# Down projections of a feed-forward stage: which engine forms the weight block differences and adds the residuals

## The reference, cut to what matters

```python
x = x + rms_norm(mixed, norm_mix_post)
h = rms_norm(x, norm_ffn_pre)
f = (jax.nn.silu(h @ w_gate) * (h @ w_up)) @ w_down
x = x + rms_norm(f, norm_ffn_post)
# rms_norm(x, g) = x * rsqrt(mean(x * x, axis=-1) + EPS) * g
```

## Time and profile before

| | |
|---|---|
| median of 3 runs | 2623.14 us (2622.61 to 2630.82) |
| the profiled execution's own time | 2624.92 us |
| its span | 2623.1 us |
| TensorE busy | 2398.5 us, 91% |
| VectorE busy | 1660.0 us, 63% |
| ScalarE busy | 1204.3 us, 46% |
| GpSimd busy | 847.5 us, 32% |
| mean granted TensorE clock | 0.968 |

### The profile page before, as it was taken

One profiled execution on the slowest core, in us unless ns is written; L12 is line 12 of the kernel. 1 busy time (PEld: TensorE's weight loads), 2 busy tenths in 40 slices (PEclk: granted clock), 3 DMA queues, 4 the chain that ended last, 5 costly groups with the idle time before them and its releaser, 6 DMA issues. The chain is left out here.

```text
span 2623.1 us, 36658 instructions
## 1 busy us (share of the span) xinstructions
PE 2398.5 (91%) x11796; PEld 1986.3 (76%) x11796; DVE 1660.0 (63%) x2987; ACT 1204.3 (46%) x2731; POOL 847.5 (32%) x912
## 2 busy tenths in 40 slices
PE   7999988996888888799589999999999999999896
PEld 5888876885776767577468888888878888888785
DVE  5676775554888888333265556558776455456877
ACT  5555563332676666333243333335444333334353
POOL 1323322222565665344401111135210111114623
PEclk9999998997999999899799999999999999999998
DMA  5111122444132221465452323256664332327663
GB/s 174 45 51 55 51 77 83 131 131 154 58 101 77 76 77 34 165 216 198 148 228 89 116 97 108 81 178 224 232 241 149 103 114 89 117 81 261 230 230 118
DMA packets 222105, 340.08 MB, mean 130 GB/s; under 512 B 20320, under 2 KB 119648, under 8 KB 220128
## 3 DMA queue, kind: packets, MB, share of 16 engines
q1 hardware_dynamic: 221920, 337.86, 38.6%
HBM read 234.50 MB, written 103.28 MB: 129 GB/s over the span
## 5 line engine op out<-in xcount | busy, mean ns | idle before, releaser
L2402 PE MATMUL ff_psum<-ff_hop,ff_a_hi 128*128 128x512 f32 x1760 | 543.3, 390 | 4.8 <-issue 4.8
L2402 PEld LDWEIGHTS ff_psum<-ff_hop,ff_a_hi 128*128 128x128 f32 x1760 | 330.8, 188 | 75.0 <-issue 6.4
L2402 PE MATMUL ff_psum<-ff_hop,ff_a_lo 128*128 128x512 f32 x880 | 342.8, 390 | 0.0
L2426 PE MATMUL ff_psum<-ff_a_hi 128*128 128x512 f32 x616 | 243.1, 395 | 14.4 <-DVE ff_a_lo L2213 14.3
L2029 POOL TENSOR_TENSOR ff_go<-ff_go 128x512 f32<-128x512 f32 x22 | 28.4, 1291 | 669.4 <-DVE ff_go L2279 669.4
L2426 PE MATMUL ff_psum<-ff_a_lo,ff_a_hi 128*128 128x512 f32 x616 | 241.4, 392 | 0.0
L2426 PE MATMUL ff_psum<-ff_a_hi,ff_a_lo 128*128 128x512 f32 x616 | 241.4, 392 | 0.0
L2213 DVE TENSOR_TENSOR ff_a_lo<-ff_ring,ff_a_hi 128x512 fp32r<-128x512 f32 x220 | 207.7, 969 | 51.2 <-ACT ff_a_hi L2100 51.2
L2100 ACT ACTIVATE ff_a_hi<-ff_w_raw 128x512 fp32r<-128x512 f32 x220 | 137.7, 628 | 211.3 <-PE ff_psum L2402 189.1
L2402 PE MATMUL ff_psum<-hop,ff_a_hi 128*128 128x512 f32 x704 | 217.8, 391 | 17.0 <-DVE ff_a_lo L2213 17.0
L1222 ACT ACTIVATE da_probs<-da_psum,da_bias 128x512 f32<-128x512 f32 (+3 forms) x320 | 196.1, 622 | 72.9 <-DVE da_bias L1274 60.8
(11 more groups left out here) (235 smaller groups left out, 5492.8 us busy)
## 6 DMA issues: line engine op xcount, KB each, us to landing
g_s<-ff_go SPq DMA_DIRECT2D x154, 256.0 KB, 2.0
ff_ring<-g_s SPq DMA_DIRECT2D x154, 256.0 KB, 3.0
ff_ring<-in_w_down_dram SPq DMA_DIRECT2D x132, 256.0 KB, 3.7
ff_w_raw<-in_w_gate_dram SPq DMA_DIRECT2D x44, 512.0 KB, 3.6
ff_w_raw<-in_w_up_dram SPq DMA_DIRECT2D x44, 512.0 KB, 4.1
pp_x<-in_x_dram SPq DMA_DIRECT2D x32, 512.0 KB, 4.6
hop_s<-op_ht SPq DMA_DIRECT2D x8, 1792.0 KB, 7.6
ff_hop<-hop_s SPq DMA_DIRECT2D x10, 1024.0 KB, 9.9
```

The costliest lines, as they stand in the source:

```text
L2402: last = pe.matmul(ps[:, bank, :], w[:, unit % R, at], hop[i][:, h, c, :], start=(i in (0, 1, 6) and c == 0 and x_ == 0), stop=(c == 3 and ...
L2426: last = pe.matmul(ps[:, bank, :], g[:, unit % R, at], w[:, (unit + 1) % R, :], start=(i in (0, 1, 6) and c == 0 and x_ == 0), stop=(c == ...
```

## The change

`b_of` moves unchanged from GpSimd to VectorE, and is called in VectorE's down step `t` for step `t + 4`, after the two low parts of that step. `add_x` moves to VectorE as well. VectorE's extras no longer stand in runs of neighbouring steps: in pass 0 `hop_half` goes to steps 24, 26, 28, 30 and 59 to 62; in pass 1 `norm` of `y_back` to steps 12, 16, 20, 24 and its `add_x` to 14, 18, 22, 26; `norm` of `y2` to 63, 65, 69, 71 and its `add_x` to 64, 68, 70, 72; the four bank additions after step 43 go one to a step. ScalarE's squares of `y_back` go from steps 14 to 17 to steps 6 to 9, and so SyncE's loads of `y_back` and `x_back` stand after step 10 in place of 12; the stores of `y_back` stand after step 40 in place of 38, the loads for steps 59 to 62 after step 64 in place of 68. At the end of a pass two of the four stores of `y2` come behind the loads of step 76. In the last group the gain row is multiplied in beforehand (`scale`: the right half in steps 73 to 76, the left half after the last matmul), so that one scalar_tensor_tensor per tile, `y1 * rstd + x`, is left behind the reciprocal root.

```diff
@@ SyncE, down(p)
-                        if p == 1 and t == 12:
+                        if p == 1 and t == 10:
                             ...
-                        if p == 1 and t == 38:
+                        if p == 1 and t == 40:
                             store_rows(b.y_back, 0, 0, 1)
-                        if p == 0 and t == 68:
+                        if p == 0 and t == 64:
                             ...
-                    store_rows(y2, p, 1, 2 * p)
+                    store_rows(y2, p, 1, 2 * p, (0, 1))
                     load_step(p, DOWN - 1)
+                    store_rows(y2, p, 1, 2 * p, (2, 3))
@@ GpSimd (b_of and add_x removed)
-                    for t in range(NJ, 5 * NJ):
-                        b_of(p, t)
-                        if p == 1 and t == 27:
-                            rstd_of(1)
-                        if p == 1 and 28 <= t < 32:
-                            add_x(b.y_back, b.x_back, 1, t - 28)
+                    if p == 1:
+                        rstd_of(1)
                     rstd_of(2 * p)
-                    for k in range(4):
-                        add_x(y2, b.x_in, 2 * p, k)
@@ VectorE
+                def add_x(y, x, group, k):
+                    dve.wait_ge(x_loaded, 64 * group + 64)
+                    dve.wait_ge(y_normed, 4 * group + k + 1)
+                    dve.tensor_tensor(y[:, k, :], y[:, k, :], x[:, k, :], ALU.add).then_inc(x_added, 1)
+                def scale(n, k):
+                    at = slice(n * HT, (n + 1) * HT)
+                    dve.wait_ge(squared, 12 + 4 * (1 - n) + k + 1)
+                    dve.tensor_tensor(y1[:, k, at], y1[:, k, at], post_row[:, at], ALU.mult).then_inc(y_scaled, 1)
@@ VectorE, down_step(p, t), behind lo_until
+                    if NJ <= t + 4 < 5 * NJ:
+                        b_of(p, t + 4)
+                    if p == 1 and t in (12, 16, 20, 24):
+                        norm(b.y_back, 1, (t - 12) // 4)
+                    if p == 1 and t in (14, 18, 22, 26):
+                        add_x(b.y_back, b.x_back, 1, (t - 14) // 4)
+                    if t in (63, 65, 69, 71):
+                        norm(y2, 2 * p, (63, 65, 69, 71).index(t))
+                    if t in (64, 68, 70, 72):
+                        add_x(y2, b.x_in, 2 * p, (64, 68, 70, 72).index(t))
+                    if p == 1 and t >= 73:
+                        scale(1, t - 73)
@@ VectorE, behind the last bank additions
                 for k in range(4):
-                    norm(y1, 3, k)
-                    if k % 2 == 1:
-                        dve.wait_ge(last_x_loaded, 64)
-                        dve.wait_ge(y_normed, 12 + k + 1)
-                        dve.tensor_tensor(y1[:, k, :], y1[:, k, :], b.x_back[:, k, :], ALU.add).then_inc(dve_x_added, 1)
+                    scale(0, k)
+                    dve.wait_ge(rstd_ready, 3 + k + 1)
+                    dve.wait_ge(y_scaled, 4 + k + 1)
+                    dve.scalar_tensor_tensor(y1[:, k, :], y1[:, k, :], rstd[:, k:k + 1], b.x_back[:, k, :], ALU.mult, ALU.add)\
+                        .then_inc(x_added, 1)
```

More of the change, by code:

```diff
@@ L1817, in ffn @@
         squared, pool_step, rstd_ready = m.sem("squared"), m.sem("pool_step"), m.sem("rstd_ready")
-        y_normed, x_loaded, x_added, dve_x_added = (m.sem(n) for n in ("y_normed", "x_loaded", "x_added", "dve_x_added"))
+        y_normed, x_loaded, x_added, y_scaled = (m.sem(n) for n in ("y_normed", "x_loaded", "x_added", "y_scaled"))
         last_x_loaded = m.sem("last_x_loaded")
@@ L1955, in load_x, with store_rows @@
                         sp.dma_start(tile[:, k, :], x_mid[row(p, h, k):row(p, h, k) + P, :]).then_inc(semaphore, 16)
-                def store_rows(tile, p, h, group):
-                    for k in range(4):
+                def store_rows(tile, p, h, group, rows=range(4)):
+                    for k in rows:
                         sp.wait_ge(x_added, 4 * group + k + 1)
@@ L2013, in _ @@
                 for k in range(4):
-                    sp.wait_ge(*((x_added, 12 + k // 2 + 1) if k % 2 == 0 else (dve_x_added, k // 2 + 1)))
+                    sp.wait_ge(x_added, 12 + k + 1)
                     sp.dma_start(out[row(1, 0, k):row(1, 0, k) + P, :], y1[:, k, :]).then_inc(last_stored, 16)
@@ L2037, in a_of @@
                     pool.tensor_tensor(go[:, S4, :], go[:, C21, :], go[:, S2, :], ALU.subtract).then_inc(go_made, 1)
[L2039 to L2052, removed]
                 def rstd_of(group):
@@ L2058, in rstd_of @@
                     pool_rstd(pool, rstd[:, :], ss[:, 0, :], D, half[:, :], pool_step, group + 1).then_inc(rstd_ready, 1)
[L2060 to L2063, removed]
                 for p in range(PAIRS):
@@ L2084, in _ @@
                         .then_inc(rstd_ready, 1)
-                for k in (0, 2):
-                    add_x(y1, b.x_back, 3, k)
             @block.scalar
@@ L2164, in down_step @@
                             act.activation(to, ps[:, 4 + k, :], ACT.Copy).then_inc(y_copied, 1)
-                    if p == 0 and 24 <= t < 28:
-                        hop_half(1, 2 + (t - 24) // 2, t % 2)
-                    if p == 1 and 14 <= t < 18:
+                    if p == 0 and t in (24, 26, 28, 30):
+                        hop_half(1, 2 + (t - 24) // 4, (t - 24) // 2 % 2)
+                    if p == 1 and 6 <= t < 10:
                         act.wait_ge(y_loaded, 64)
-                        square(b.y_back, 1, t - 14)
+                        square(b.y_back, 1, t - 6)
                     if 57 <= t < 61:
@@ L2172, in down_step @@
                         square(y2, 2 * p, t - 57)
-                    if p == 0 and 67 <= t < 71:
-                        hop_half(1, (t - 67) // 2, (t - 67) % 2)
+                    if p == 0 and 59 <= t < 63:
+                        hop_half(1, (t - 59) // 2, (t - 59) % 2)
                     if p == 1 and 69 <= t < 73:
@@ L2221, in hop_half, with b_of @@
                         .then_inc(hop_split[i], 1)
+                def b_of(p, t):
+                    i, c = divmod(t, NJ)
+                    raw = ring[:, 2 * ring_at[t] + 1, :]
+                    dve.wait_ge(*step_at(p, t))
+                    if i in (1, 2):
+                        dve.wait_ge(*step_split(p, t - NJ))
+                        dve.tensor_tensor(keep[:, c, :], raw, keep[:, c, :], ALU.subtract).then_inc(b_made, 1)
+                    elif i == 3:
+                        dve.wait_ge(b_made, 4 * NJ * p + t - 2 * NJ + 1)
+                        dve.tensor_tensor(raw, keep[:, c, :], raw, ALU.subtract).then_inc(b_made, 1)
+                    else:
+                        dve.wait_ge(*step_split(p, t - 2 * NJ))
+                        dve.wait_ge(b_made, 4 * NJ * p + t - 2 * NJ + 1)
+                        dve.tensor_tensor(keep[:, c, :], raw, keep[:, c, :], ALU.subtract).then_inc(b_made, 1)
                 def s_of(p, j, x, v):
@@ L2292, in norm @@
                         dve.wait_ge(post_loaded, 16)
-                    dve.wait_ge(rstd_ready, group + 1 if group < 3 else 3 + k + 1)
+                    dve.wait_ge(rstd_ready, group + 1)
                     dve.scalar_tensor_tensor(y[:, k, :], y[:, k, :], rstd[:, k:k + 1], post_row[:, :], ALU.mult, ALU.mult)\
                         .then_inc(y_normed, 1)
+                def add_x(y, x, group, k):
[6 more added lines that the diff above has]
+                    dve.tensor_tensor(y1[:, k, at], y1[:, k, at], post_row[:, at], ALU.mult).then_inc(y_scaled, 1)
                 def add_c11(p, k):
@@ L2303, in down_step @@
                         up_slot(p, NJ - 1, 14 + t)
[L2304 to L2307, removed]
+                    if 4 * NJ <= t < 4 * NJ + 4:
+                        k = t - 4 * NJ
+                        dve.wait_ge(y_copied, 12 * p + 8 + k + 1)
+                        add_bank(y2[:, k, HT:D], k).then_inc(y_added, 1)
                     if t in (5 * NJ, 5 * NJ + 1):
```

1 line of the change is left out of this document (added).

## The result

The changed kernel takes 2593.62 us (median of 4 runs, 2591.81 to 2595.19), the kernel before 2625.89 us (4 runs, 2622.61 to 2630.82): ratio 0.988, 95% interval 0.9863 to 0.9898, so 27 to 36 us faster. The forecast was 2597 (2592 to 2605). The profiled execution took 2592.32 us, its span is 2590.5.

What follows compares the result with a forecast made beforehand. TensorE was taken as the bound, waiting in the down parts for VectorE's low parts; 21.0 us there plus 4.9 in the tail off the profiled 2624.92 gave 2599.0, less 1.8 for the median: 2597 us (2592 to 2605).

Steps and rivals of the forecast that it cites:

- The size of the loss: In the two down parts: time TensorE loses against its undisturbed pace, 6.0 and 15.0 us, all 21.0 us gained back.
- VectorE carries the load: In the down steps: VectorE takes the differences at 0.60 us each within 4.1 us of slack, cost 0.
- The queue move: Pass 1, earlier y_back and x_back loads: VectorE stands 3.7 us for step 11's load, 1.0 to spare, TensorE 0.
- The tail: After the last matmuls: first bank addition to last operation takes 11.5 us instead of 16.4, gain 4.9 us (3.3 to 6.5).
- the distance per tile: In the tail: time from one tile's last operation to the next, taken as 2.5 us (bounds 1.8 to 3.05).
- extras apart: Down parts: VectorE's side jobs no longer in neighbouring steps, counted within the 21.0 us gain without a price of its own.
- Rival B: Down parts: work moved from GpSimd still burdens VectorE, waits stay, only the tail gains, 2618 us; chance 0.05.
- A: Step 11 of pass 1 or hop halves of steps 59 to 62 land late: 1.8 to 6 us, 2601; chance 0.20.
- D: Pass 1: loads and VectorE wait for each other in a loop, 5 to 12 us, 2603 to 2609; chance 0.09.
- C: Down steps: VectorE becomes the bound at 3.15 us a step against 2.73, 37 us more, 2655; chance 0.04.

Runs made afterwards that it cites:

- e4: Changed kernel with 2.1 MB more loaded behind x_back and ahead of step 11 of pass 1; median 2602.91 us, ratio 0.9913 to the kernel before.
- e6: Changed kernel with one constant subtraction more on VectorE at each of its 88 differences; ratio 0.9901 to the kernel before.
- e1: Kernel before with the block differences moved to VectorE, norms still in neighbouring steps, additions still on GpSimd, tail as before; ratio 0.9975 to the kernel before.
- e2: Changed kernel with the block differences left on GpSimd and the tail as before; ratio 0.9926 to the kernel before.
- e5: Changed kernel with 88 more constant-block subtractions on GpSimd that nobody waits for; ratio 1.0022 to the kernel before.
- e10: Changed kernel with norms and x additions of y_back and y2 put back in neighbouring steps, both on VectorE; ratio 0.9918 to the kernel before.
- e7: Changed kernel with two constant subtractions more on VectorE at each of its 88 differences; ratio 1.0128 to the kernel before.

## Why the prediction was right

**The size of the loss: right.** 21.0 us were read from the pace, 22.3 came back. The difference is the pace itself, 0.2267 us a matmul in place of the 0.2275 taken from the chain. Reading it from starts and not from the 14.3 us of waits was what mattered: the slow starts behind waits were real time (e4: 4.95 us waited, 7.0 lost). The text did not say that they are the granted clock at 0.50; they are 4.4 us of the kernel before, and most of the rest beyond 14.3 is what the count of waits leaves out at each wait.

**VectorE carries the load: right.** 0.60 us by starts for a difference, no TensorE wait in either pass. e6 shows the room: one operation more a step costs 6.2 us, two 63.

**The queue move: right to 0.1 us.** The wait of VectorE was forecast at 3.7 us and is 3.78; TensorE was to have 1.0 to spare and had 0.7, and e4 shows that it was that near.

**The tail: right in kind, short in size.** 4.9 forecast, 5.7 measured. The mis-sized term is the distance per tile: 2.5 taken, 2.0 measured (2583.29 to 2585.29), 1.5 us less over three. With one 0.6 and one 1.2 us operation of VectorE a tile, GpSimd's held operations still fit between. Half of it was made up by another miss: the first of these operations starts at 2579.30, 3.4 us behind the first bank addition in place of the 2.7 taken, since `scale` of tile 0 stands ahead of it.

**What the text got wrong is the share.** It laid VectorE's lateness to GpSimd's operations and listed "extras apart" beside them without a price. The table of two by two gives it: in neighbouring steps the norms and additions lose 10.1 us with no GpSimd beside; e1, with GpSimd beside and its other differences, loses 18.8, 4.5 of them by the clock; apart, who adds makes 0.4 us. The differences' move bought 3.7 us alone (e1), the rest of the change 16.7 (e2). Rival B (port load is conserved, only the tail gains) is refuted by the changed kernel; the hold it rests on exists (e5), but moving a GpSimd operation of 1.3 to 1.7 us to VectorE costs VectorE 0.6. A and D did not come true, C not with this load.

**The median** came 3.4 us under the forecast: 1.3 of it from the down parts, 0.8 from the tail, the rest, 1.3, from the scatter of the stages ahead. That it came so near is in part luck: the profiled execution was forecast at 2599.0 and took 2592.3, 4.4 us of which are scatter, and the start alone scatters by 9 us. The forecast's own range, 2594 to 2599, was just missed.

## What to carry to other kernels

Judge an engine that feeds TensorE by its load in each step against its slack, not by its busy share: VectorE was busy 63% of the span before and after, and yet TensorE lost 22 us in a few steps where VectorE's side jobs stood in a row. Setting such jobs apart cost no time here and gave most of this gain; taking away the neighbour engine's operations that hold it matters where there is no slack left to hide them. When a wait for a transfer moves into the stream of the feeding engine, work out landing time against deadline: here the spare time was 0.7 us, and 2.1 MB more in the queue cost 7 us.

## What was not expected of the hardware

Operations that nobody waits for can cost more than useful ones: GpSimd's 88 idle subtractions lost 34 us (e5). The clock fell to 0.50 behind waits of about 2 us in one kernel and not behind waits as long in another (e1 and e10), and it never fell in e7, with 81 waits of up to 1.4 us; the three falls in the kernel before are 4.4 of its 22.3 us. The stages ahead of the feed-forward, with identical code, end anywhere within 9 us (1311.9 to 1320.9) from profile to profile. The traces show TensorE itself slower there: up to 1311 us its same 6252 matmuls are busy 1123.8 us in the changed kernel and 1131.8 in e1, and the clock stood at 0.50 for 127 us in the one and 154 in the other ahead of the start. Whether that is the cause or a result of other delays is not settled, since no run here varies those stages.
